# Six places instead of eight for the side work in the two-chain scan of an RWKV-7 and differential-attention kernel

## What is computed

```python
def rwkv7_recurrence(r, w, k, v, a, b):
    """S_t = S_{t-1} diag(w_t) + (S_{t-1} a_t) b_t^T + v_t k_t^T ;  y_t = S_t r_t."""
    def step(S, inp):
        r_t, w_t, k_t, v_t, a_t, b_t = inp
        Sa = jnp.einsum('bhvk,bhk->bhv', S, a_t)
        S = S * w_t[:, :, None, :] + Sa[..., None] * b_t[:, :, None, :] + v_t[..., None] * k_t[:, :, None, :]
        y = jnp.einsum('bhvk,bhk->bhv', S, r_t)
        return S, y
    S0 = jnp.zeros((Bn, H, N, N), jnp.float32)
    _, y = lax.scan(step, S0, (tm(r), tm(w), tm(k), tm(v), tm(a), tm(b)))
```

## Time and profile before

| | us |
|---|---|
| median of 3 runs (1749.82 to 1750.33) | 1750.26 |
| the profiled execution | 1748.08 |
| its span in the trace | 1746.2 |
| PE busy | 1608.3 (92%) |
| DVE busy | 788.6 (45%) |
| ACT busy | 636.1 (36%) |
| POOL busy | 638.5 (37%) |

### The profile page before, as it was taken

How to read it: one execution, slowest core, us unless ns; L and a number is a source line. 1 busy time by engine, 2 the same in 40 slices (tenths; PEclk the granted TensorE clock), 3 DMA queues, 4 the chain that set the end, 5 groups by cost and what they waited for, 6 DMA issues and landing times. The chain is left out here.

```text
span 1746.2 us, 20826 instructions
## 1 busy us (share of the span) xinstructions
PE 1608.3 (92%) x7503; PEld 1276.4 (73%) x7503; DVE 788.6 (45%) x1241; ACT 636.1 (36%) x1063; POOL 638.5 (37%) x309
## 2 busy tenths in 40 slices
PE   4799993879989999999999979998899999999998
PEld 3566683879937878888887767765567888888877
DVE  4866948673345532013213767357545320132133
ACT  4655433445543422122224343336724221122242
POOL 4233233334322344434433425352223343344442
PEclk8899996899989999999999999998999999999999
DMA  4112200002011233322223233220002223322221
GB/s 129 58 63 73 72 25 0 2 15 98 2 48 37 84 96 101 104 96 96 96 97 103 83 112 97 73 72 25 1 24 97 96 96 108 96 96 97 96 80 65
DMA packets 123462, 127.17 MB, mean 73 GB/s; under 512 B 8316, under 2 KB 120060, under 8 KB 123384
## 3 DMA queue, kind: packets, MB, share of 16 engines
q1 hardware_dynamic: 122720, 124.90, 21.9%
q0 software_dynamic: 288, 0.63, 0.2%
q10 hardware_dynamic: 376, 0.61, 0.1%
HBM read 124.00 MB, written 2.12 MB: 72 GB/s over the span
## 5 line engine op out<-in xcount | busy, mean ns | idle before, releaser
L419 POOL TENSOR_TENSOR wlo<-wraw,whi 128x2048 fp32r<-128x2048 f32 (+1 forms) x111 | 506.6, 4564 | 866.4 <-ACT whi L1167 796.2
L572 PE MATMUL pb<-xh,whi 128*128 128x512 f32 x1184 | 476.2, 402 | 27.2 <-DVE xl L1669 14.6
L573 PE MATMUL pb<-xl,whi 128*128 128x512 f32 x1184 | 465.7, 393 | 0.0
L574 PE MATMUL pb<-xh,wlo 128*128 128x512 f32 x1184 | 465.5, 393 | 0.0
L572 PEld LDWEIGHTS pb<-xh,whi 128*128 128x128 f32 x1184 | 224.7, 190 | 101.0 <-issue 38.1
L1167 ACT ACTIVATE whi<-wraw 128x2048 fp32r<-128x2048 f32 (+1 forms) x111 | 209.2, 1884 | 235.7 <-PE pb L574 235.5
L573 PEld LDWEIGHTS pb<-xl,whi 128*128 128x128 f32 x1184 | 225.2, 190 | 48.0 <-issue 3.4
L574 PEld LDWEIGHTS pb<-xh,wlo 128*128 128x128 f32 x1184 | 225.0, 190 | 47.7
L572 PE MATMUL pb<-hid_h,whi 128*128 128x512 f32 x512 | 202.4, 395 | 0.0
L574 PE MATMUL pb<-hid_h,wlo 128*128 128x512 f32 x512 | 202.3, 395 | 0.0
L573 PE MATMUL pb<-hid_l,whi 128*128 128x512 f32 x512 | 202.3, 395 | 0.0
(11 more groups left out here) (275 smaller groups left out, 2032.3 us busy)
## 6 DMA issues: line engine op xcount, KB each, us to landing
wraw<-in_mlp_w_dram SPq DMA_DIRECT2D x128, 512.0 KB, 4.3
wraw<-in_rwkv_w_rkvo_dram SPq DMA_DIRECT2D x32, 512.0 KB, 4.4
wraw<-in_ple_w_gate_dram SPq DMA_DIRECT2D x16, 512.0 KB, 4.4
xtok<-in_x_dram SPq DMA_DIRECT2D x8, 512.0 KB, 6.0
wraw<-in_w_k_shared_dram SPq DMA_DIRECT2D x8, 512.0 KB, 4.0
wraw<-in_w_v_shared_dram SPq DMA_DIRECT2D x8, 512.0 KB, 4.4
wraw<-in_diff_w_q_dram SPq DMA_DIRECT2D x8, 512.0 KB, 4.0
wraw<-in_diff_w_o_dram SPq DMA_DIRECT2D x8, 512.0 KB, 4.4
```

What stands on the lines that cost most here:

```text
L419: pool.tensor_tensor(wlo[:, par, rng], wraw[:, par, rng], whi[:, par, rng].bitcast(F32), ALU.subtract).then_inc(s.w_lo, 1)
L572: mm(o, wh, ah, start=first, stop=False)
L573: mm(o, wh, al, start=False, stop=False)
L574: return mm(o, wl, ah, start=False, stop=last)
```

## The change

Only the table in fill changes. k_score and lower_times, which were two calls of two units each, become one call of four units, in the first of the two places that each had. The last transpose moves from place 6 to 5, the corner product from 7 to 6. Places 2 and 7 are left empty.

```diff
                 if slot == 0:
                     turn(q, 0)
                 elif slot == 1:
-                    k_score(q, 0, 2)
-                elif slot == 2:
-                    k_score(q, 2, 4)
+                    k_score(q, 0, 4)
                 elif slot == 3:
                     turn(q, 1)
                 elif slot == 4:
-                    lower_times(q, 0, 2)
+                    lower_times(q, 0, 4)
                 elif slot == 5:
-                    lower_times(q, 2, 4)
+                    turn(q, 2)
                 elif slot == 6:
-                    turn(q, 2)
-                else:
                     corner(q)
```

## The result

| | before | after |
|---|---|---|
| median of 4 runs each, us | 1750.04 | 1768.20 |
| lowest and highest | 1748.24, 1750.33 | 1767.11, 1769.97 |
| the profiled execution | 1748.08 | 1769.97 |
| its span | 1746.2 | 1768.0 |

The change makes the kernel slower: the ratio is 1.0107, with a 95% interval of 1.0089 to 1.0124. That is 18.2 us by the medians and 21.8 us by the spans of the two profiled executions. The forecast was 1772.5 us in a range of 1762 to 1788.

The account below looks back on a forecast made before the run. PE's own work was taken to bound the late scan, DVE most early steps. Waits of 7.3 + 1.3 + 7.7 + 1.2 = 17.5 us plus 4.8 us of clock gave 22.3 us, so 1772.5 us, range 1762 to 1788.

Parts of the forecast that it names:

- What bounds the scan: Scan: PE's own work bounds 400 to 478 us, DVE most steps before 393; delay goes straight to the program's end.
- The wait for Vtok: Late odd steps, nine: with corner gone from the z_turn to values_in gap, each grows by 0.88 us.
- Corner has its input in the late steps: Late steps: Xbd is made before corner's new place, so no new wait there.
- The merging itself: lower_times as one call gains 0.07 us per period, range 0 to 0.15; k_score gains nothing.
- Even steps: Late even steps, eight: z_turn of chain 1 waits 0.16 us for Zt, 1.3 us in all; early ones nothing.
- Early odd steps: k = 3 to 11, five: PE waits for Xbd ahead of corner; 1.55 us each, 7.7 us in all.
- shift: Early odd steps: all of lower_times ahead of answer(1, k-1) makes everything on DVE 0.42 us later.
- The clock: Scan: three more low-clock stretches of some 3.4 us at 1.6 us each, 4.8 us.
- The sum over 14 periods: Whole forecast loss: 17.5 us of waits and 4.8 us of clock, 22.3 us.
- the early periods absorb it: Rival: DVE, bounding steps 2 to 12, makes up PE's loss, only the late part pays; 1760 us, 12%.
- Only PE's own work counts: Rival: chains have slack, merging saves 0.07 to 0.15 us in each of 15 periods; 1749 us, 6%.
- The clock falls in nearly every period: Rival: idle and narrow work lower the clock in nearly every period; 1790 us, at half of them 1779; 15%.

Follow-up runs that it names:

- e6: Kernel before, with only the corner product and last transpose one place earlier, nothing merged: 1763.18 us, ratio 1.0083.
- e1: Changed kernel, with ACT's copy to Vtok in odd steps moved ahead, between take_u(0, k) and take_y(0, k): 1756.53 us, ratio 1.0047.
- e5: Changed kernel, with the corner product put back behind z_turn of chain 1 (place 7), still six places: 1753.05 us, ratio 1.0030.
- e2: Kernel before, with only k_score merged in place 1 and place 2 empty: 1747.49 us, ratio 0.9998.
- e9: Changed kernel, with PE idle time filled by useless matmuls in empty place 7 and ahead of corner in steps 3 to 11: 1765.85 us, ratio 1.0090.
- e3: Kernel before, with only lower_times merged in place 4 and place 5 empty: 1747.18 us, ratio 1.0004.

## Why the prediction was right, point by point

- **What bounds the scan:** right. The late half was full of PE's own work, the early half hung on DVE, and the delay went to the end.
- **The wait for Vtok:** right, in mechanism and size. z_turn and values_in stayed 1.14 us apart. Forecast for a late odd step 0.88 us, measured by e6 0.85. e1 and e5 took the wait away from either side and most of the loss went with it.
- **Corner has its input in the late steps:** right, no wait for Xbd there.
- **The merging itself:** the 0.07 us taken off per period weren't there; of 1.04 us, e2 and e6 leave -0.01.
- **Even steps:** 0.16 forecast, 0.20 measured by e2. Together 0.97 forecast for a late period and 1.04 measured.
- **Early odd steps:** forecast were 1.55 us each. e9, the changed kernel nearly without low clock, shows what the waits alone cost. In the three early periods where it has no low clock and before at most 0.1 us (those of k = 3, 9 and 11) the growth was 1.34, 1.37 and 1.47 us. The term that was mis-sized is the "shift" of 0.42 us, which was put in full on five steps: from the start of the period to Xbd it came to 0.22, 0.22 and 0.32. e3 fits that: 0.17, -0.04 and 0.05 us for lower_times alone, where by its rows above Nbd no longer ran beside DVE's inverse (the -0.04 in spite of 3.9 us at the lower clock). For k = 11, Xbd starts 385.11 - 375.59 = 9.52 us into the period in before and 393.29 - 383.45 = 9.84 us into it in e9:

```profile
375.59 0.60 PE L715 MATMUL pb<-cst,Bbd 128*128 128x128 f32 x4
...
385.11 0.42 DVE L1858 TENSOR_TENSOR Xbd<-pb,cst 128x256 f32<-128x256 f32 x1
```

```profile
383.45 0.60 PE L715 MATMUL pb<-cst,Bbd 128*128 128x128 f32 x4
...
393.29 0.42 DVE L1862 TENSOR_TENSOR Xbd<-pb,cst 128x256 f32<-128x256 f32 x1
```

The other part holds. In after at k = 11 corner came 0.48 us behind DVE's start on Xbd, z_turn 1.87 and values_in 3.00 behind it, against 0.48, 1.85 and 2.99 forecast, counted from the same start.
- **The clock:** the direction was right, the size not. Forecast were three more stretches of 3.4 us at 1.6 us each, 4.8 us. Measured were two more stretches, but each twice as long, 24.3 us more at the lower level in all; at the 0.29 us per us of e9 that is about 7.0 us. The price of 1.3 to 1.7 us per 3.4 us was taken too high (by e9 it is 1.0): it was reckoned from PE's rate alone, on 18 or 19 records per stretch where the earlier trace rows have 17 to 19, and where PE waits for DVE anyway a slower PE costs little. The length was taken too low.
- **The sum over 14 periods:** measured 22.8 us. The late seven give 7.3, against 6.8 forecast. The first seven give 15.5, of which 7.0 is clock by the price above and 8.5 is waits. For the same seven, waits of 1.2 + 7.7 + 0.8 = 9.7 us and 4.8 us of clock had been forecast. So 1.2 us too much for waits stood against 2.2 us too little for the clock, and that these nearly cancelled was luck.
- **The rivals:** "the early periods absorb it" fell, since they grew by 15.5 us. "Only PE's own work counts" fell by the wait of 0.86 us. "The clock falls in nearly every period" came true in the early half, at k = 3, 5, 7, 9 and 12, at a lower price, and not at all in the late half. What the Trainium skill, page "TensorE: Matmul & The Clock Gate", section "A second HAM failure mode: psum-queue depth-cycling", tells, that short idle times between groups swing the clock, is borne out by the early half alone.
- **Against the median:** 22.3 us forecast, 21.8 by the spans and 18.2 by the medians. The traced execution of before lay 2.0 us under its median and that of after 1.8 us over it; with one trace of each, where in the program these 3.8 us lie is not shown. The scan itself grew by more than the span did, 22.8 us in 14 of its 15 periods, so the near hit on 21.8 is in part chance.

## What to carry to other kernels

A gap in a dependent chain is worth filling only with work that is as long as the slowest thing the gap waits for, and that can be a copy queued behind another one on the reading engine, not the chain's own latency. So before side work is moved, read for each gap what ends it, including the order of the engine that answers. Here moving one copy in ACT's program was worth more than any order on PE that was tried, and the longer side product belonged where the longest answer was due.

## What the runs showed of the hardware beyond what was expected

- In the scan, five low-clock stretches in a row lasted 6.8 us and not 3.4 us. Four of them (k = 3, 5, 7, 9) began within 2 us of the narrow corner product, which had an idle time of 1.5 to 2.5 us ahead of it and the wait of 0.86 us for Vtok behind it; the fifth (k = 12) began 1.4 us behind an idle time of 1.96 us ahead of z_turn, with neither beside it. At k = 11 the same pattern as in the four, with 1.13 us ahead of corner, passed without a fall. The late periods, with idle times of about 0.9 us in 11, kept the upper level throughout. A full us at the lower level cost 0.29 us of time in the early half on average, and between 0 and 0.5 by the period.
- A DVE product of 128x184 took 0.76 us beside a POOL instruction and 0.35 us alone, one of 128x58 0.68 and 0.22. So where POOL's work falls against DVE's can pay for most of a delay of DVE: 0.26 of 0.44 us at k = 9 and 0.39 of 0.44 at k = 11.
